# Eight modulation pieces moved from the second mixer to the place behind the experts

## The reference, cut

```python
def first_block(x, ...):
    for l in range(2):
        x = x + token_mixers(rmsnorm(x, mix_norm_g[l]), ...)
        h = rmsnorm(x, ffn_norm_g[l])
        x = x + (swiglu(h, ...) if l == 0 else moe_ffn(h, ...))
    return rmsnorm(x, final_norm_g)

def second_block(x, c, ...):
    c_act = silu(c)
    for l in range(2):
        mod = c_act @ ada_w[l] + ada_b[l]          # 1024 x 6144
        shift_m, scale_m, gate_m, shift_f, scale_f, gate_f = split(mod, 6)
        h = rms_norm(x, g_pre_mix[l]) * (1 + scale_m) + shift_m
        ...
```

## Time and profile before

| | us |
|---|---|
| median of 3 runs | 2143.86 |
| lowest and highest | 2143.04, 2145.4 |
| span of the profiled execution, first to last instruction | 2141.1 |
| PE busy in it | 2086.2 |
| DVE, ACT, POOL busy | 1551.3, 1192.2, 49.0 |

### The profile page before, as it was taken

How to read it: one execution, slowest core, us unless ns; L and a number is a source line. 1 busy time by engine, 2 the same in 40 slices (tenths; PEclk the granted TensorE clock), 3 DMA queues, 4 the chain that set the end, 5 groups by cost and what they waited for, 6 DMA issues and landing times.

```text
span 2141.1 us, 25645 instructions
## 1 busy us (share of the span) xinstructions
PE 2086.2 (97%) x10570; PEld 1707.1 (80%) x10570; DVE 1551.3 (72%) x1534; ACT 1192.2 (56%) x1267; POOL 49.0 (2%) x89
## 2 busy tenths in 40 slices
PE   7999999999999999999999999999979999999998
PEld 6877778887877678888888888888867788787887
DVE  5766766556767769999898989999866554566444
ACT  5544354446544357777777777777734444345443
POOL 0000000000000000000000000000000000000000
PEclk9999999999999999999999999999979999899999
DMA  9676665555666669999999999999963575435551
GB/s 312 232 260 219 253 225 193 191 182 199 233 237 247 246 196 343 357 365 367 347 366 365 362 345 366 366 367 367 368 231 99 164 252 185 131 107 174 183 194 59
DMA packets 370071, 549.04 MB, mean 256 GB/s; under 512 B 21270, under 2 KB 295574, under 8 KB 363030
## 3 DMA queue, kind: packets, MB, share of 16 engines
q1 hardware_dynamic: 365488, 536.53, 73.5%
q10 hardware_dynamic: 4460, 10.80, 1.4%
HBM read 546.13 MB, written 1.15 MB: 256 GB/s over the span
## 4 chain that ended last, share of the span: by engine, by line
PE 92%; DVE 5%; ACT 2%; issue 1%; DMA 0%; POOL 0%; SPq 0%; POOLq 0%; DVEq 0%; ACTq 0%
PE bank L454 86%; PE bank L482 2%; PE bank L541 2%; DVE wlo L1123 1%; ACT whi L1116 1%; DVE xn L1684 1%; DVE gate_tanh L1680 0%; PE bank L581 0%; DMA raw<-in_w_in 0%; PE bank L571 0%; DVE scoresB L1694 0%; PE bank L953 0%; DVE xn L2067 0%; DVE x L2057 0%; PE bank L547 0%
## 5 line engine op out<-in xcount | busy, mean ns | idle before, releaser
L1123 DVE TENSOR_TENSOR wlo<-raw,whi 128x2048 fp32r<-128x2048 f32 x459 | 1046.5, 2286 | 368.5 <-ACT whi L1116 366.4
L1116 ACT ACTIVATE whi<-raw 128x2048 fp32r<-128x2048 f32 x459 | 877.6, 1914 | 429.1 <-PE bank L454 348.1
L454 PE MATMUL bank<-whi,hThi 128*128 128x512 f32 (+2 forms) x1088 | 430.5, 396 | 12.7 <-DVE hTlo L1609 5.4
L454 PE MATMUL bank<-whi,hTlo 128*128 128x512 f32 (+2 forms) x1088 | 423.0, 389 | 0.0
L454 PE MATMUL bank<-wlo,hThi 128*128 128x512 f32 (+2 forms) x1088 | 422.8, 389 | 0.0
L454 PE MATMUL bank<-whi,slots_hi 128*128 128x512 f32 x704 | 274.4, 390 | 0.0
L454 PE MATMUL bank<-whi,slots_lo 128*128 128x512 f32 x704 | 274.3, 390 | 0.0
L454 PE MATMUL bank<-wlo,slots_hi 128*128 128x512 f32 x704 | 274.0, 389 | 0.0
L454 PEld LDWEIGHTS bank<-whi,hThi 128*128 128x128 f32 x1088 | 209.7, 193 | 79.3 <-issue 30.4
L454 PEld LDWEIGHTS bank<-whi,hTlo 128*128 128x128 f32 x1088 | 209.9, 193 | 41.5
L454 PEld LDWEIGHTS bank<-wlo,hThi 128*128 128x128 f32 x1088 | 210.0, 193 | 39.0 <-issue 0.5
(11 more groups left out here) (317 smaller groups left out, 2279.3 us busy)
## 6 DMA issues: line engine op xcount, KB each, us to landing
raw<-in_moe_w SPq DMA_DIRECT2D x352, 512.0 KB, 6.6
raw<-in_moe_w SPq DMA_DIRECT2D x88, 1024.0 KB, 8.4
raw<-in_w_in SPq DMA_DIRECT2D x72, 1024.0 KB, 7.2
raw<-in_ada_w SPq DMA_DIRECT2D x48, 1024.0 KB, 7.1
raw<-in_ffn_w SPq DMA_DIRECT2D x44, 512.0 KB, 4.9
raw<-in_w_gate SPq DMA_DIRECT2D x44, 512.0 KB, 4.0
raw<-in_w_up SPq DMA_DIRECT2D x44, 512.0 KB, 5.0
raw<-in_w_down SPq DMA_DIRECT2D x22, 1024.0 KB, 4.9
```

Of the source, the lines that this page charges most:

```text
L454: m = mm(dst, l_, r_, start=start and i == 0, stop=stop and i == len(pairs) - 1)
L1116: s.then_inc(s.unit.activation(split_slots(p)[0][:, 0:n], slot_of_ring(raw, p, NRAW)[:, 0:n], ACT.Copy), ("hi", p), sem="weights_hi")
L1123: e.then_inc(e.unit.tensor_tensor(lo[:, 0:n], slot_of_ring(raw, p, NRAW)[:, 0:n], hi[:, 0:n].bitcast(F32), ALU.subtract), ("lo", p), sem=sem)
```

## The change

The eight pieces `d16` to `d23` of the second layer (its third chunk) leave the second mixer. They are done behind the experts, on PE ahead of `second_mixer(0)`. The `kv2` piece is taken ahead of them in the plan. The row of that chunk is made by ACT behind the second half's features of the second block; it is put into a row of `probT`, since `rowbuf` belongs to the first block, and a wait is added where `probT` is written next. The second mixer's DVE wait for the last row becomes a wait for the one before it.

```diff
--- before.py
+++ after.py
@@ -432,6 +432,7 @@
 
 
         mod_chunks = [[(l, c, k) for c in range(MOD // PIECE) for k in range(KD)] for l in range(DEPTH)]
+        behind_experts = mod_chunks[1][2 * KD:]
         last_chunk = {l: (l, MOD // PIECE - 1) for l in range(DEPTH)}
 
 
@@ -897,6 +898,9 @@
                 for step in behind_chunks:
                     run(step)
 
+            def keys_piece(l):
+                return piece(("kv2", l), full_piece(a["w_in2"][l], 512))
+
             def second_mixer(l, here):
                 w = a["w_in2"][l]
 
@@ -923,12 +927,13 @@
                 v_bank = t.take(("v2", l))
                 features(xn3, here, lambda tt, k: ("modulated", l, 0, tt), (0,))
                 t.ahead = 0
-                read, parts = piece(("kv2", l), full_piece(w, 512))
+                read, parts = held.pop(("kv2", l), None) or keys_piece(l)
                 wf = full(parts)
                 values(0)
                 features(xn3, here, lambda tt, k: ("modulated", l, 0, tt), (1,))
                 t.ahead = AHEAD
                 t.look_ahead()
+                t.split_ahead(("q2", l, 0), 1)
                 t.then_inc(values(1), ("full", ("v2", l)))
                 bank = t.take(("k2", l))
                 t.then_inc(project_features(wf, 0, here, bank, 0), ("full", ("k2", l)), read)
@@ -1053,7 +1058,7 @@
             t.wait_ge("first_tables")
             for l in range(DEPTH):
                 for step in MIXER_T[l]:
-                    if l == 0 or step not in ("d0", "d1"):
+                    if l == 0 or not (step in ("d0", "d1") or step[0] == "d" and mod_chunks[1][int(step[1:])] in behind_experts):
                         mixer_step(l, step)
                 t.ahead = AHEAD
                 def turn_second(tt, half):
@@ -1084,7 +1089,10 @@
                 else:
                     experts_router(l)
                     two_ways(t, lambda: sparse_experts(l), lambda: dense_experts(l))
-                    t.ahead = AHEAD
+                    t.ahead = 0
+                    held["kv2", 0] = keys_piece(0)
+                    for z in behind_experts:
+                        modulation_piece(*z)
             for l in range(DEPTH):
                 def turn_modulated(tt, half):
                     if half == 0:
@@ -1174,7 +1182,7 @@
             return pairs[:, :, 0, :], pairs[:, :, 1, :]
 
         ys_of = lambda nt: [(tt, hf) for tt in range(nt) for hf in range(2)]
-        mod_row = rowbuf[32:33, :]
+        mod_row = lambda l, c: (probT if l and c == 2 else rowbuf)[32:33, :]
 
 
         def scalar_program(s):
@@ -1202,10 +1210,10 @@
             def modulation_row(l, c):
                 s.wait_ge(("full", ("mod", l, c)), row_of_chunk[0])
                 for j in range(4):
-                    s.then_inc(act(mod_row[:, half_of(j)], s.bank(("mod", l, c))[32 * j:32 * j + 1, :], ACT.Copy),
+                    s.then_inc(act(mod_row(l, c)[:, half_of(j)], s.bank(("mod", l, c))[32 * j:32 * j + 1, :], ACT.Copy),
                                *([("free", ("mod", l, c))] if j == 3 else []))
                 s.own()
-                s.then_inc(load(mod_raw[l:l + 1, c * PIECE:(c + 1) * PIECE], mod_row), ("row_out", l, c), sem="modulation_row_out", by=16)
+                s.then_inc(load(mod_raw[l:l + 1, c * PIECE:(c + 1) * PIECE], mod_row(l, c)), ("row_out", l, c), sem="modulation_row_out", by=16)
                 row_of_chunk[0] = "row_out", l, c
 
             def collect_modulation(l):
@@ -1333,9 +1341,9 @@
                         s.then_inc(act(tok3(gv)[:, tt], bank[:, 0:MIX], ACT.Copy), *([("gv", l)] if tt else []))
                         side(("p3v", l), bank, gr, MIX, tt)
                 elif kind[0] == "d":
-                    l_, c, k = mod_chunks[l][int(kind[1:])]
-                    if k == KD - 1:
-                        modulation_row(l_, c)
+                    at = mod_chunks[l][int(kind[1:])]
+                    if at[2] == KD - 1 and at not in behind_experts:
+                        modulation_row(l, at[1])
                 elif kind[0] == "g" and kind[1] != "l" and n[1] == "b":
                     b, hf = int(kind[1]), int(n[0])
                     s.wait_ge(("merged", l, b - 2) if b >= 2 else None)
@@ -1481,7 +1489,7 @@
                                    scale=col("pool_scale", l, g_)), *([("poolw_hi", l, g_ // 2)] if g_ % 2 else []))
                 for h2 in range(QH // 2):
                     name = "probT", l, 1, h2
-                    s.wait_ge(("full", name))
+                    s.wait_ge(("full", name), ("row_out", 1, 2))
                     s.then_inc(act(probT_[1][:, 2 * h2:2 * h2 + 2, :], s.bank(name)[:, :].rearrange("p (j n) -> p j n", j=2), ACT.Copy),
                                ("free", name), *([("probT", l, 1)] if h2 == QH // 2 - 1 else []))
                 s.split_ahead(("wout2", l, 1), 1)
@@ -1556,6 +1564,7 @@
             square_sum(xn3[:, 1], 1, 3, ("squares", "modulated", 0, 0, 1))
             load_attention(0)
             features((0, "mix2"), None, (1,))
+            modulation_row(1, 2)
             load_gate(0, 0)
             load_shift_and_scale(0, 1)
             load_gate(0, 1)
@@ -2279,7 +2288,7 @@
                     scaled_by_root(l + 1, "mix", (1,))
                     features((l + 1, "mix"), lambda k: col("mix_g", l + 1, k), (1,))
                 else:
-                    v.wait_ge(("row_out", *last_chunk[l]))
+                    v.wait_ge(("row_out", l, 1))
                     router_tokens(l, 0)
                     scaled_by_root(l, "ffn", (0,))
                     add_to_x(l, "mix", lambda tt, hf: (("wout", l, hf), tt), [(1, 1)])
```

## The result

| | before | with the change |
|---|---|---|
| median, us (12 runs each, same chip) | 2143.19 | 2149.17 |
| lowest to highest | 2140.68 to 2145.45 | 2148.22 to 2154.43 |
| span of the profiled execution | 2141.1 | 2147.3 |
| PE busy in it | 2086.2 | 2090.4 |

The ratio is 1.0027, with a 95% interval of 1.0019 to 1.0036. The change costs 6.0 us. That lies inside the range of the prediction, 1.1 us under its upper end, but the change is clear of noise, and the forecast was +2.3.

The account below looks back on a forecast made before the run. PE, in flight for 97% of the span, was taken as the bound. Mixer -4.2, hole +7.5 and clock -1.0 gave +2.3 us on the median 2143.86, so 2146.2, with a range of 2140.5 to 2150.3.

Parts of the forecast that it names:

- The mixer's 4.2 us: Second mixer: taking out the eight pieces gains 4.2 us on PE's path, out of their 7.96.
- The hole's 7.5 us: Between experts and second block: doing the eight pieces there makes the transposes begin 7.5 us later.
- The clock's 1.0 us: Behind the moved pieces: a higher granted clock for one half's transposes saves 1.0 us of a possible 7.8.
- rival B: Behind the experts the full clock comes back and stays: -2.7 us in sum, 2141.2; chance 0.15.
- ACT's row at 0: Second block, behind the second half's features: four ACT copies, 2.44 us, hidden in 4.4 us of room, cost 0.
- A: Behind the experts the pieces themselves run at the low clock, about 1.9 us each: +5.7 us, 2149.6; chance 0.16.
- D: Behind the experts PE's jump ends only at 1567.5 or later, the hole stays unfilled: +4.8 us, 2148.7; chance 0.09.
- slower by over 0.2%: Whole kernel measurably slower than before: A, half of D and the forecast's upper edge, chance 0.24.

Follow-up runs that it names:

- one_piece: Changed kernel with only `d16` done behind the experts and `d17` to `d23` left out; 2139.73 us, 0.9981 of the kernel before.
- same_slot: Changed kernel with all eight products kept, the last three pieces rereading the raw slot of `d20` instead of their own loads; 2142.67 us.
- filler_in_gaps: Changed kernel with useless matmuls on constants, 7 ahead of `d22` and 6 ahead of `d23`; 2148.47 us.
- the filler runs: filler_in_gaps, and the kernel before with 11 useless matmuls on constants behind the experts, 2142.25 us.
- spread_slots: Changed kernel with three pieces behind the experts, five in the second block's first mixer, `d12` to `d15` in the second mixer's free places; 2141.41 us.

## Why the prediction was right or wrong

- **The mixer's 4.2 us: right.** 3.9 by the trace without the dip, 3.35 by `one_piece`. `d20`, `d22`, `d23` gave nothing and left the pauses named; at `d19` PE waited 0.81 us, and at `d21` it gained the full 1.0. What was 0.3 short is a wait of 0.31 us for DVE's `ylo` ahead of the first level scores, once `d18` was gone.
- **The number: inside the range by its width.** 2149.17 lies under the upper end, 2150.3, but the sum gave 2146.2. The three terms missed by 0.3, 2.8 and 0.6 us, all to the same side, and the range held that only since it had been drawn wide for the rivals. That the number is inside is in part luck.
- **The hole's 7.5 us: the step that failed.** Measured 10.3. Its sentences were "PE begins at 1565.0", 3.44 us behind its last matmul, and "PE does them from 1565.0 to 1570.0 at 1.0 us". PE began 4.07 us behind it, and in the ten later runs that have work there 3.8 to 5.2: the step took DVE's jump for PE's. The pieces began at the low level, the first three at some 1.7 to 1.9 us each. `d16` was so read 6.0 us behind the experts' end and not 4.4, and its slot's next load was issued at 1565.72; it took 4.8 us, against 4.9 in the sum. No wait shows for it: the pieces ahead of it were slow too, and six stand back to back. But `d22` was ready 14.6 us after the experts' end, not 12.2; `d23` 17.2, not 15.1; and it then took 1.9 us at the low level, not 1.1. That is the 2.8 us: 0.6 for the restart, 1.4 for the slots and transfers behind slow pieces, 0.8 for `d23`. Why `d22`'s load was issued only at 1569.0, some 1.6 us after `d17` should have been read, the traces don't settle.
- **The clock's 1.0 us: 0.4, and not from the transposes that it was taken from.** These ran at the low level (1.97 us); T to Q was 0.4 us shorter all the same. I read the values' slow rows as "it did not rise" and left the fast case to rival B. In fact the clock rose at 1569.2 and fell again. That the moved pieces have idle times between them was in the prediction, and that these are what costs the clock is shown by `same_slot` and `filler_in_gaps`. The Trainium skill's rule ("TensorE: Matmul & The Clock Gate", section "What's actually happening"), that the throttled clock is the default and activity releases it, is borne out by the filler runs, where matmuls without use raise the mean granted clock from 0.985 to 0.988 and 0.987; but released is not kept: it fell again at 1576.0 here and at 1581.9 in `filler_in_gaps`, and a microsecond at the full clock is a microsecond of the span only where nothing else is late.
- **ACT's row at 0: right**, but of the 4.4 us of room 4.0 were used and not the 2.4 of the sum. The four copies took 2.43 us and the store behind them is issued by ACT as well, so the split began 6.9 us behind the second transposes (1593.36), not 3.3. DVE had the low half at 1597.7, PE wanted it at 1598.05.
- **The rivals.** A (the pieces run at the low clock, +5.7) came nearest in size, and half of it happened: the first three pieces ran low and the last one, not all eight. Its own price took the transfers as hidden. B would have needed PE without pauses. D's restart was late by 0.6 us, not by 2.5.
- **The chances.** I gave "slower by over 0.2%" 0.24. The hole's sum had been built on the best value for three unknown costs at once (restart, speed of the pieces, clock of the last), all of which could only move one way.

## What to carry to other kernels

A hole in an engine's timeline isn't as wide as it looks: take off the restart, and price the filling at the clock that the engine has when it restarts, not at the one of the place from which the work comes. Three pieces fitted here, eight did not. Moved work whose operands come by DMA should need no slot that the work itself must first free, since each such wait costs twice, once as idle time and once as clock. And when a faster stretch gives nothing in the end, look at the next transfer in a neighbour's queue: most of the gain of this case came only after ACT's loads had been moved out of the way, a move that on the old kernel was worth nothing.

## What the runs showed of the hardware

- The mean granted clock of whole executions told apart kernels whose times overlap: 0.985 for the kernel before, also with ACT's loads moved, and for `one_piece`; 0.987 to 0.989 for the nine others. It says nothing of work and waits: the changed kernel has 0.985 as well and is 6.0 us slower.
- In several executions the granted clock fell for about 3.4 us while PE was busy without a pause (592 to 597 us above, at 0.66 on average), at a place that differed between executions or was missing. That one cost 1.6 us: the same instructions of DVE and ACT are 0.23 us later than in the kernel before at 589 us and 1.80 later at 679. So one profiled execution can't be compared with another to better than that without looking for them.
- The same loads of `pool_weights` (256 KB, issued by ACT) took 5.3 us to land before the change and 16.4 us in `spread_slots`, where 381 GB/s moved between T and Q (258 before).
- PE's restart behind the joined branch varied from 3.8 to 5.2 us between runs. The Trainium skill ("Runtime: NRT & Kernel Launch", section "Instruction fetch mechanics") says that branching breaks the sequential prefetch of instructions, and that a taken branch to a target outside the pages held has to fetch it first; no run here separates that from other causes.
